# Encoder step on eight cores: the residual add moved to GpSimd, later norm sums and taps, and a DMA transpose of the second group's input

## The chip, the cores and the metric

One program runs on all 8 cores of one Trainium2 chip, each core on its own half of a stream and two of the sixteen running streams; the cores exchange nothing. The metric is the device time of the slowest core in microseconds (us). Engines: TensorE (PE; PEld is its weight load), VectorE (DVE), ScalarE (ACT), GpSimd (POOL), SyncE (SP, which here only issues DMAs).

## What is computed

```
x = x + rmsnorm(merged @ w_out, g_mix_post)          # merged = [normed pooling | normed gated conv]
x = x + rmsnorm(cross_attn(rmsnorm(x, g_x_pre), mem_k, mem_v, w_q, w_co), g_x_post)
hid = jnp.square(jax.nn.relu(rmsnorm(x, g_ff_pre) @ w_up))
x = x + rmsnorm(hid @ w_down, g_ff_post)
```

ahead of it `proj = rmsnorm(x, g_mix_pre) @ w_in`, split into `u | B | C | h`. Pooling: four groups of 128 channels of `u` are averaged over trailing windows of 2, 4, 8, 16 rows, less `u`, and mapped by a 128x128 matrix each. Convolution: `B * conv3(C * h)`, three taps over time per channel. Both are normed by group (128 and 64 channels). The model width is 1024, the hidden width 4096. A core has 2048 prompt rows and 32 rows of running streams.

## The kernel before, in words

The 2048 rows are done in two groups of 8 blocks of 128 rows (`grp` 0 and 1; group 0 has the 32 running rows, `SMP`, as well). A group goes through stage A (`w_in`, mixing), `out_block` with `w_out` for each block, attention (queries, scores, then `out_block` again with the product of values and `w_co`), `w_up`, and `w_down`. Weights come as 512-column pieces into a ring of 6 buffers, loaded through the GpSimd queue as buffers come free.

Order is the order in which the Python code adds instructions: each engine runs its own list in that order, and semaphores are derived from overlaps of what is read and written. A unit is 8 matmuls of one output tile; `tick()` follows it, and `later(n, f)` runs `f` at the n-th tick from then (one more when called outside a tick). So a step put later by one unit stands behind 8 more matmuls on TensorE and behind everything those units add on the others.

Stage A has four phases, each one quarter of `w_in`: U (16 units in group 0), then C, h and B of 12 units each (group 0: three column tiles by four channel groups). `pool_ops` queues the window sums, which are popped after each unit (`pool_some`); `MAP_AT` says after which unit (phase, unit) each pooled tile is mapped (`pool_map`: a matmul into a PSUM bank, a square on ScalarE, then `norm_fin`: the matmul of the norm sums, Ln and Exp on ScalarE, and one tick later a `stt` on VectorE that reads the map's bank and frees it). `bank()` hands out six PSUM banks, the one picked longest ago first. `conv_b` is one tap of the convolution; `conv_some` pops one. `mix_B` multiplies by B and asks for the norm sums of its tile with `later(2, ...)`; `sq_slot` is the buffer of the squares.

`out_block` has 16 matmuls of 512 columns into a pair of banks. Then ScalarE squares the pair with a sum (into `junk`, the bytes of `O`) and makes the factor 1/rms (`rstd`: Ln, Exp); VectorE multiplies by the gain (`tt` into `O`) and adds `O` times the factor to the residual `X` (`stt`). Two ticks later `pre_a` does the next norm: a square of `X` with a sum into `xs`, `rstd`, and the scaling, on ScalarE for every other block and on VectorE for the rest; `pre_b` three ticks later turns it on TensorE (8 transposes) and VectorE puts it into `xT` with its gain.

`stage_down` does the two halves of `w_down` one after the other; `down_evac` ends each block, and in the first half of group 0 `hook0` prepares the 8 blocks of the second group, 8 transposes on TensorE each. A program prints the functions here:

## Time and profile before

| | us |
|---|---|
| three runs, median (lowest to highest) | 898.75 (897.88 to 900.32) |
| the profiled execution | 901.45 |
| its span on the slowest core, core 1 | 900.1 |
| spans of the other cores | 893.8 to 898.5 |
| TensorE busy, core 1 | 859.5 (95%) |
| VectorE, ScalarE, GpSimd busy, core 1 | 448.9, 432.4, 53.0 |

Times in views count from the start of a core's span. Stages of core 1: stage A to 104.5, `w_out` blocks to 142, attention to 262, `w_up` to 380, `w_down` to 475; then the second group, whose stage A ends near 563, its `w_out` blocks near 591, attention near 670. A TensorE that is busy is running matmuls, at the clock granted (PEclk, 1.00 is 2.4 GHz). GpSimd's busy time is only the issue of DMAs.

### The profile page before, as it was taken

What the parts mean: (1) busy time and instruction counts of PE and PEld (TensorE: products, weight loads), DVE (VectorE), ACT (ScalarE), POOL (GpSimd) and SP (SyncE); (2) the same over time, 40 slices, a digit from 0 to 9 for tenths busy, and PEclk for the clock granted to TensorE, in tenths of its full rate; (3) what the DMA queues carried; (4) which work ended last, traced back from release to release, by engine and by line L of the source; (5) the groups of instructions that cost most, each with busy time, mean ns of one, the idle gap of its engine ahead of it and who ended that gap; (6) DMA issues with size and microseconds to landing.
All of it is one profiled execution on the core that took longest, in us unless ns stands there. A gap on an engine that the chain in (4) does not pass through costs nothing.

```text
span 900.1 us, 14693 instructions; the slowest of 8 cores (893.8 to 900.1 us)
## 1 busy us (share of the span) xinstructions
PE 859.5 (95%) x5018; PEld 453.0 (50%) x5018; DVE 448.9 (50%) x772; ACT 432.4 (48%) x1043; POOL 53.0 (6%) x66
## 2 busy tenths in 40 slices
PE   7898898999999999999999998999899999999996
PEld 4565444664456666544444443457454444444442
DVE  3788687476872222232142877886684222200133
ACT  4557888466873333332132386886684333200122
POOL 1100100000000000000001000000000000000000
PEclk9989989999999999999999999999999999999998
DMA  9997376719585654636829992171716746426022
GB/s 195 194 155 110 76 118 105 127 28 206 76 151 81 98 80 62 102 88 115 117 100 120 236 228 82 40 96 23 95 21 110 107 69 94 59 36 87 8 94 94
DMA packets 66793, 91.89 MB, mean 102 GB/s; under 512 B 2936, under 2 KB 58360, under 8 KB 66208
## 3 DMA queue, kind: packets, MB, share of 16 engines
q0 software_dynamic: 58080, 60.95, 48.1%
q1 hardware_dynamic: 8640, 30.00, 10.2%
q8 instruction: 42, 0.69, 0.3%
q14 instruction: 31, 0.25, 0.1%
HBM read 137.49 MB, written 12.30 MB: 166 GB/s over the span
## 4 chain that ended last, share of the span: by engine, by line
PE 80%; ACT 9%; issue 4%; DVE 4%; DMA 2%; ACTq 0%; DVEq 0%; SPq 0%; POOLq 0%
PE psum L393 77%; PE psum L397 3%; ACT stg L411 3%; ACT xsb L411 3%; ACT st L411 2%; ACT un L411 2%; DMA ring<-w_in 1%; DMA X<-xp 1%; DVE un L423 1%; DVE xT L414 1%; DMA conv_p<-stg 1%; DVE X L423 0%; DVE un L414 0%; DVE un L418 0%; DVE xsb L418 0%
## 5 line engine op out<-in xcount | busy, mean ns | idle before, releaser
L393 PE MATMUL psum<-xT,ring 128*128 128x352 bf16 (+6 forms) x2336 | 413.0, 333 | 3.6 <-DVE xT L414 2.5
L393 PEld LDWEIGHTS psum<-xT,ring 128*128 128x128 bf16 x2336 | 226.5, 98 | 167.5 <-issue 6.6
L393 PE MATMUL psum<-ring,un 128*128 128x512 bf16 (+1 forms) x1408 | 302.6, 380 | 0.0
L411 ACT ACTIVATE un<-psum 128x352 bf16<-128x352 f32 (+9 forms) x258 | 125.0, 492 | 201.2 <-PE psum L393 198.9
L393 PEld LDWEIGHTS psum<-ring,un 128*128 128x128 bf16 (+1 forms) x1408 | 130.7, 98 | 157.7 <-issue 9.1
L414 DVE TENSOR_TENSOR un<-un 128x352 bf16<-128x352 bf16 (+5 forms) x176 | 84.8, 483 | 156.8 <-ACT un L411 156.8
L414 DVE TENSOR_TENSOR stg<-psum,gp 128x1024 f32<-128x1024 f32 (+3 forms) x51 | 53.1, 1042 | 106.6 <-ACT stg L411 57.6
L411 ACT ACTIVATE stg<-psum 128x1024 bf16<-128x1024 f32 (+3 forms) x51 | 44.5, 873 | 104.8 <-PE psum L393 102.6
L414 DVE TENSOR_TENSOR xT<-psum,gcs 128x1024 bf16<-128x1024 bf16 (+2 forms) x52 | 60.0, 1155 | 35.7 <-PE psum L397 35.2
L393 PE MATMUL psum<-ring,mg 128*128 128x512 bf16 (+1 forms) x320 | 75.8, 388 | 0.0
L423 DVE SCALAR_TENSOR_TENSOR X<-stg,st,X 128x1024 f32<-128x1024 f32 (+3 forms) x51 | 56.3, 1104 | 6.8 <-DVE stg L414 4.7
L411 ACT ACTIVATE mg<-psum 128x512 f32<-128x512 f32 (+2 forms) x23 | 13.7, 596 | 87.4 <-PE psum L393 71.0
L393 PEld LDWEIGHTS psum<-ring,mg 128*128 128x128 bf16 (+1 forms) x320 | 30.4, 99 | 35.8 <-issue 7.9
L414 DVE TENSOR_TENSOR mg<-psum,gp 128x512 f32<-128x512 f32 (+1 forms) x17 | 11.6, 690 | 60.8 <-ACT mg L411 58.7
L411 ACT ACTIVATE st<-st,epsb 128x1 f32<-128x1 f32 (+2 forms) x105 | 30.9, 295 | 10.3 <-ACT un L411 0.4
L397 PE MATMUL psum<-idb,un 128*128 128x128 bf16 (+2 forms) x288 | 25.3, 217 | 10.7 <-DVE un L418 8.9
L411 ACT ACTIVATE xsb<-X 128x1024 bf16<-128x1024 f32 (+1 forms) x34 | 35.4, 1042 | 0.0
L411 ACT ACTIVATE un<-psum,ast 128x256 bf16<-128x256 f32 (+1 forms) x72 | 33.2, 470 | 1.9 <-DVE ast L430 1.9
L433 DVE TENSOR_REDUCE ast<-psum 128x2 f32<-128x512 f32 (+1 forms) x36 | 24.8, 688 | 17.9 <-PE psum L397 9.0
L397 PE MATMUL psum<-idb,xsb 128*128 128x128 bf16 (+1 forms) x336 | 25.7, 220 | 7.8 <-DVE xsb L418 5.3
L411 ACT ACTIVATE st<-st 128x1 f32<-128x1 f32 (+2 forms) x122 | 26.3, 216 | 11.8 <-ACT st L411 0.8
L397 PEld LDWEIGHTS psum<-idb,xsb 128*128 128x128 bf16 (+1 forms) x336 | 21.1, 99 | 21.0 <-issue 16.5
(95 smaller groups left out, 517.1 us busy)
## 6 DMA issues: line engine op xcount, KB each, us to landing
ring<-w_up POOLq DMA_DIRECT2D x16, 1024.0 KB, 14.2
ring<-w_down POOLq DMA_DIRECT2D x16, 1024.0 KB, 10.7
X<-xp SPq DMA_DIRECT2D x16, 512.0 KB, 14.0
yp<-X SPq DMA_DIRECT2D x16, 512.0 KB, 2.7
ring<-w_in POOLq DMA_DIRECT2D x7, 1024.0 KB, 11.4
ring<-w_out POOLq DMA_DIRECT2D x4, 1024.0 KB, 31.8
ring<-w_q POOLq DMA_DIRECT2D x4, 1024.0 KB, 22.7
stg<-xp SPq DMA_DIRECT2D x8, 512.0 KB, 4.3
```

Of the source, the lines that this page charges most:

```text
L393: P.add("pe", lambda e: e.matmul(out, lhsT=lhsT, rhs=rhs, start=start, stop=stop), reads=[lhsT, rhs], writes=[out])
L397: P.add("pe", lambda e: e.transpose(out=out, in_=in_, identity=idn), reads=[in_, idn], writes=[out])
L411: P.add("act", lambda e: e.activation(out=out, in_=in_, func=func, scale=scale, **kw), reads=rd, writes=wr)
L414: P.add("dve", lambda e: e.tensor_tensor(out=out, in0=in0, in1=in1, op=op), reads=[in0, in1], writes=[out])
L423: P.add("dve", lambda e: e.scalar_tensor_tensor(out=out, in0=in0, scalar=scalar, in1=in1, op0=op0, op1=op1), reads=rd, writes=[out])
L433: P.add("dve", lambda e: e.tensor_reduce(out=out, in_=in_, axis=mybir.AxisListType.X, op=ALU.max, negate=True), reads=[in_], writes=[out])
```

## The change

The residual `X + O * factor` is split: VectorE makes `O = psum * factor * gain` in one `stt` that now needs the factor, and GpSimd adds `O` to `X`. The scaling of `pre_a` in `out_block` is always on VectorE, its square goes to `junk`, and `pre_b` comes a tick later. In stage A the maps of group 0 stand two units apart from unit 5 of phase 1 on, their sums come 2 units later in place of 1, those of the B tiles 3 in place of 2 (both groups), with a fourth square buffer, and taps may run after every unit above 7. The factor of the last norm takes one ScalarE step less in the second half, and the last block leaves in two halves on two queues. In `hook0` the 8 turns go by DMA (SP queue) with the gain applied in place 7 ticks later.

```diff
@@ -283,7 +283,7 @@
 A_TILES = [[(14, 368), (368, 720), (720, 1072)], [(16, 528), (528, 1040)]]
 P_TILES = [[(0, 528), (528, 1072)], [(16, 528), (528, 1040)]]
 P_AT = [(12, 16), (4, 8)]
-MAP_AT = [[[(1, 8), (1, 9), (1, 10), (1, 11)], [(2, 3), (2, 5), (2, 7), (2, 9)], [(2, 11), (3, 0), (3, 2), (3, 4)]],
+MAP_AT = [[[(1, 5), (1, 7), (1, 9), (1, 11)], [(2, 1), (2, 3), (2, 5), (2, 7)], [(2, 9), (2, 11), (3, 1), (3, 3)]],
           [[(1, 4), (1, 5), (1, 6), (1, 7)], [(2, 2), (2, 3), (2, 4), (2, 5)]]]
 F_TILES = [[(16, 368), (368, 720), (720, 1072)], [(16, 528), (528, 1040)]]
 Q_TILES = [F_TILES[0], [(16, 400), (400, 784), (784, 1040)]]
@@ -547,12 +547,12 @@
 
     xs_rr = [0]
 
-    def pre_a(Xap, r, key, on_act=False, xs=None):
+    def pre_a(Xap, r, key, on_act=False, xs=None, junk=None):
         if xs is None:
             k = xs_rr[0] % 2
             xs_rr[0] += 1
             xs = xsb[0:r, k * D:(k + 1) * D]
-        act(xs, Xap, AF.Square, accum=stat(key, 3, r))
+        act(xs if junk is None else junk, Xap, AF.Square, accum=stat(key, 3, r))
         rstd(stat(key, 3, r), stat(key, 4, r), stat(key, 5, r), D)
         if on_act:
             act(xs, Xap, AF.Copy, scale=stat(key, 5, r))
@@ -597,7 +597,7 @@
     sA_OFF = S_OFF
     sB_OFF = [sA_OFF + 16 * w for w in SW]
     SQ_OFF = [sB_OFF[g] + 12 * SW[g] for g in range(2)]
-    RF_OFF = [o + 3072 for o in SQ_OFF]
+    RF_OFF = [SQ_OFF[0] + 3072, SQ_OFF[1] + 4096]
     U3 = uf(U_OFF, 4 * UW).rearrange("p (g t) -> p g t", g=4)
     V3 = uf(V_OFF, 4 * VW).rearrange("p (g t) -> p g t", g=4)
     Z3 = uf(U_OFF, 4 * MW).rearrange("p (g t) -> p g t", g=4)
@@ -689,9 +689,9 @@
             k = map_rr[0] % 4
             map_rr[0] += 1
             return stgb[:, 512 * k:512 * k + n]
-        k = sq_rr[0] % 3
+        k = sq_rr[0] % 4
         sq_rr[0] += 1
-        return ub(SQ_OFF[grp] + 1024 * k, n)
+        return mg[:, 8736:8736 + n] if k == 3 and grp == 0 else ub(SQ_OFF[grp] + 1024 * k, n)
 
     def pool_map(grp, g, lo, hi):
         l1 = max(lo, 16) - 16
@@ -701,7 +701,7 @@
         mm(out, wpool[:, g * 128:(g + 1) * 128], PL3[:, g, l1:h1], True, True)
         sq = sq_slot(grp, n, True)
         act(sq, out, AF.Square, scale=pvt[:, g:g + 1])
-        later(1, lambda: norm_fin(grp, sq, n, ones, 128, out, psg[:, g:g + 1], mg3[:, g, l1:h1]))
+        later(2 if grp == 0 else 1, lambda: norm_fin(grp, sq, n, ones, 128, out, psg[:, g:g + 1], mg3[:, g, l1:h1]))
 
     def conv_a(grp, cc):
         act(Z3[:, cc, 0:NB * 128], V3[:, cc, 0:NB * 128], AF.Copy, scale=WCO(0, cc))
@@ -723,7 +723,7 @@
         tt(y, ps, y, ALU.mult)
         sq = sq_slot(grp, n)
         act(sq, y, AF.Square)
-        later(2, lambda: norm_fin(grp, sq, n, bd64, 64, y, GCO(cc), mg3[:, 4 + cc, lo - 16:hi - 16]))
+        later(3, lambda: norm_fin(grp, sq, n, bd64, 64, y, GCO(cc), mg3[:, 4 + cc, lo - 16:hi - 16]))
 
     def state_out(grp, src, n, dst):
         ms = stg[0:n, D:D + 512]
@@ -801,7 +801,7 @@
                 fill(ph, n, len(units))
                 tick()
                 pool_some(2 if ph == 0 else 1)
-                if grp == 1 or ph == 3 or n % 2 == 1:
+                if grp == 1 or ph == 3 or n % 2 == 1 or n > 7:
                     conv_some()
                 if ph == 3 and n == 3:
                     if grp == 0:
@@ -852,20 +852,19 @@
             if h == 0:
                 weave()
                 tick()
-        par = o_rr[0] % 2 == 0
         k = o_rr[0] % 2
         o_rr[0] += 1
         O = stg[0:r, k * D:(k + 1) * D]
         junk = stgb[0:r, k * 2 * D:k * 2 * D + D]
         act(junk, ps, AF.Square, accum=stat(key, 0, r))
         rstd(stat(key, 0, r), stat(key, 1, r), stat(key, 2, r), D)
-        tt(O, ps, gp[0:r, :], ALU.mult)
+        stt(O, ps, stat(key, 2, r), gp[0:r, :], ALU.mult, ALU.mult)
         xb = Xs(blk)
-        stt(xb, O, stat(key, 2, r), xb, ALU.mult, ALU.add)
+        P.add("pool", lambda e: e.tensor_tensor(out=xb, in0=xb, in1=O, op=ALU.add), reads=[xb, O], writes=[xb])
 
         def p2():
-            xs = pre_a(xb, r, key, par)
-            later(3, lambda: pre_b(xs, r, gi, xT3[:, :, c0 + 16:c0 + 16 + r]))
+            xs = pre_a(xb, r, key, False, None, junk)
+            later(4, lambda: pre_b(xs, r, gi, xT3[:, :, c0 + 16:c0 + 16 + r]))
         later(2, p2)
         weave()
         tick()
@@ -1141,24 +1140,30 @@
         if h == 0:
             O = obuf(b)
             act(O, ps, AF.Square, accum=stat(key, 6, r))
+            act(stat(key, 6, r), stat(key, 6, r), AF.Identity, scale=1.0 / D, bias=epsb[0:r, 0:1])
             tt(O, ps, gp[0:r, 0:512], ALU.mult)
             return
         k = o_rr[0] % 2
         o_rr[0] += 1
         O = stg[0:r, k * D:k * D + 512]
         act(O, ps, AF.Square, accum=stat(key, 7, r))
-        act(stat(key, 0, r), stat(key, 6, r), AF.Identity, bias=stat(key, 7, r))
-        rstd(stat(key, 0, r), stat(key, 1, r), stat(key, 2, r), D)
+        act(stat(key, 1, r), stat(key, 7, r), AF.Ln, scale=1.0 / D, bias=stat(key, 6, r))
+        act(stat(key, 2, r), stat(key, 1, r), AF.Exp, scale=-0.5)
         tt(O, ps, gp[0:r, 512:1024], ALU.mult)
         xb = Xs(b)
 
         def fin():
             stt(xb[:, 0:512], obuf(b), stat(key, 2, r), xb[:, 0:512], ALU.mult, ALU.add)
+            r0 = 0 if b == SMP else (grp * NB + b) * 128
+            last = grp == 1 and b == NB - 1
+            if last:
+                dma("act", yp[r0:r0 + 128, 0:512], xb[:, 0:512], wr=False)
             stt(xb[:, 512:1024], O, stat(key, 2, r), xb[:, 512:1024], ALU.mult, ALU.add)
             if b == SMP:
                 dma("sp", ysm[:, :], xb, wr=False)
+            elif last:
+                dma("sp", yp[r0:r0 + 128, 512:1024], xb[:, 512:1024], wr=False)
             else:
-                r0 = (grp * NB + b) * 128
                 dma("sp", yp[r0:r0 + 128, :], xb, wr=False)
         fin()
 
@@ -1287,7 +1292,9 @@
             xs = pre_a(sl, 128, 12 + j % 2)
             if j + 2 < NB:
                 dma("sp", sl, xrow(1, j + 2), rd=False)
-            later(2, lambda: pre_b(xs, 128, 0, xT3[:, :, xcol(j):xcol(j) + 128]))
+            dst = xT3[:, :, xcol(j):xcol(j) + 128]
+            P.add("sp", lambda e: e.dma_start(out=dst, in_=xs, transpose=True), reads=[xs], writes=[dst], dma=True)
+            later(7, lambda: tt(dst, dst, gcs[:, 0:8].unsqueeze(2).to_broadcast([128, 8, 128]), ALU.mult))
 
     def cache_loads():
         for mc in range(2):
```

TensorE in phase 1 of group 0 (the C units of 8 matmuls 128x352; `un,wpool` is a map, `stg,ones` its norm sums), before:

```order
L393 MATMUL psum<-xT,ring 128x352 x40
L393 MATMUL psum<-un,wpool 128x352
L393 MATMUL psum<-xT,ring 128x352 x8
L393 MATMUL psum<-un,wpool 128x352
L393 MATMUL psum<-stg,ones 128x352
L393 MATMUL psum<-xT,ring 128x352 x8
L393 MATMUL psum<-un,wpool 128x352
L393 MATMUL psum<-stg,ones 128x352
L393 MATMUL psum<-xT,ring 128x352 x8
L393 MATMUL psum<-un,wpool 128x352
```

and in the changed kernel:

```order
L393 MATMUL psum<-xT,ring 128x352 x16
L393 MATMUL psum<-un,wpool 128x352
L393 MATMUL psum<-xT,ring 128x352 x16
L393 MATMUL psum<-un,wpool 128x352
L393 MATMUL psum<-stg,ones 128x352
L393 MATMUL psum<-xT,ring 128x352 x16
L393 MATMUL psum<-un,wpool 128x352
L393 MATMUL psum<-stg,ones 128x352
L393 MATMUL psum<-xT,ring 128x352 x16
L393 MATMUL psum<-un,wpool 128x352
```

The first map stands three units earlier, and a bank is now asked for again between units 9 and 10. VectorE's list is the same up to the first two `mg<-psum` steps that free maps' banks.

VectorE in the `w_out` stage of group 0 (`stg` is `O`, `xsb` the scaled rows, `xT` the turned rows), before:

```order
L414 TENSOR_TENSOR stg<-psum,gp 128x1024
L423 SCALAR_TENSOR_TENSOR X<-stg,st,X 128x1024
L418 TENSOR_SCALAR xsb<-X,st 128x1024
L414 TENSOR_TENSOR xT<-psum,gcs 128x8x128
L414 TENSOR_TENSOR stg<-psum,gp 128x1024
L423 SCALAR_TENSOR_TENSOR X<-stg,st,X 128x1024
L414 TENSOR_TENSOR xT<-psum,gcs 128x8x128
L414 TENSOR_TENSOR stg<-psum,gp 32x1024
L423 SCALAR_TENSOR_TENSOR X<-stg,st,X 32x1024
```

and in the changed kernel:

```order
L423 SCALAR_TENSOR_TENSOR stg<-psum,st,gp 128x1024
L418 TENSOR_SCALAR xsb<-X,st 128x1024
L423 SCALAR_TENSOR_TENSOR stg<-psum,st,gp 128x1024
L414 TENSOR_TENSOR xT<-psum,gcs 128x8x128
L418 TENSOR_SCALAR xsb<-X,st 128x1024
L423 SCALAR_TENSOR_TENSOR stg<-psum,st,gp 32x1024
```

One long step a block is gone from VectorE, and the scaling stands there for every block. SyncE's queue in the `w_down` stage of group 0, as a difference:

```order
-L440 DMA stg<-xp 128x1024 x8
+L440 DMA stg<-xp 128x1024 x3
+L1296 DMA_TRANSPOSE xT<-xsb 128x8x128
+L440 DMA stg<-xp 128x1024
+L1296 DMA_TRANSPOSE xT<-xsb 128x8x128
+L440 DMA stg<-xp 128x1024
```

Each transpose stands behind the load of a later block, and both wait for the scaling of the same block.

## Rows read from the trace of the kernel before

**Rows 1.** The page: busy time by engine, and the TensorE clock in slices.
```profile
PE 859.5 (95%) x5018; PEld 453.0 (50%) x5018; DVE 448.9 (50%) x772; ACT 432.4 (48%) x1043; POOL 53.0 (6%) x66
...
PEclk9989989999999999999999999999999999999998
```

**Rows 2.** TensorE (PE) waits, core 1: line waited for, us in total, times, longest.
```profile
PE psum L397 <- DVE un L418: 8.9, 8, 3.2
PE psum L393 <- ACT un L411: 6.7, 8, 1.8
PE psum L397 <- DVE xsb L418: 5.3, 4, 1.5
...
PE psum L397 <- ACT xsb L411: 2.1, 2, 1.7
```

**Rows 3.** Windows of core 1: busy us (instructions), then clock, DMA share, GB/s.
```profile
61.00:70.00 9.00, 9.00 (x53) 5.49 (x52) 5.32 (x13) 5.40 (x12) 0.87 (x1) 0.82 1.16 162
70.00:104.50 34.50, 28.23 (x182) 16.99 (x181) 28.48 (x57) 27.24 (x58) 0.87 (x1) 1.00 0.50 81
...
800.00:825.00 25.00, 25.00 (x117) 11.33 (x116) 2.77 (x4) 2.75 (x8) 1.39 (x2) 1.00 0.25 35
```

**Rows 4.** Timeline of core 3 around 60 us: start, us, engine [idle before <-releaser].
```profile
56.09 0.31 PE L393 MATMUL psum<-un,wpool 128*128 128x352 bf16 x1
...
60.26 0.80 DVE L423 SCALAR_TENSOR_TENSOR un<-un 128x512 bf16<-128x512 f32 x2
...
60.97 0.58 DVE L423 SCALAR_TENSOR_TENSOR mg<-psum,psg,xsb 128x352 bf16<-128x352 f32 x1
...
61.70 0.31 PE L393 MATMUL psum<-un,wpool 128*128 128x352 bf16 x1 [1.12 <-DVE mg L423]
```

**Rows 5.** Timeline of core 1 in a w_out stage, one block and its neighbours.
```profile
579.48 1.02 ACT L411 ACTIVATE stg<-psum 128x1024 bf16<-128x1024 f32 x1 [0.20 <-PE psum L393]
579.65 0.75 DVE L418 TENSOR_SCALAR xsb<-X,st 128x1024 bf16<-128x1024 f32 x1
580.32 1.22 DVE L414 TENSOR_TENSOR xT<-psum,gcs 128x1024 bf16<-128x1024 bf16 x1
...
581.19 1.04 ACT L411 ACTIVATE xsb<-X 128x1024 bf16<-128x1024 f32 x1
...
581.45 1.22 DVE L414 TENSOR_TENSOR stg<-psum,gp 128x1024 f32<-128x1024 f32 x1
...
582.90 1.28 DVE L423 SCALAR_TENSOR_TENSOR X<-stg,st,X 128x1024 f32<-128x1024 f32 x1 [0.24 <-ACT st L411]
583.09 1.15 ACT L411 ACTIVATE xsb<-X,st 128x1024 bf16<-128x1024 f32 x1
```

**Rows 6.** The page, part 5: the small ScalarE instructions of rstd.
```profile
L411 ACT ACTIVATE st<-st,epsb 128x1 f32<-128x1 f32 (+2 forms) x105 | 30.9, 295 | 10.3 <-ACT un L411 0.4
...
L411 ACT ACTIVATE st<-st 128x1 f32<-128x1 f32 (+2 forms) x122 | 26.3, 216 | 11.8 <-ACT st L411 0.8
```

**Rows 7.** TensorE waits of core 1 between 530 and 563 us.
```profile
PE psum L393 <- ACT un L411: 3.0, 4, 1.6
```

**Rows 8.** Timeline of core 1, w_down of the first group, TensorE.
```profile
412.43 7.07 PE L393 MATMUL psum<-ring,un 128*128 128x512 bf16 x32
...
419.33 0.61 PE L397 MATMUL psum<-idb,xsb 128*128 128x128 bf16 x8
...
419.78 7.07 PE L393 MATMUL psum<-ring,un 128*128 128x512 bf16 x32
```

**Rows 9.** Timeline of core 1, the last block of the kernel.
```profile
893.81 0.29 ACT L411 ACTIVATE st<-st 128x1 f32<-128x1 f32 x1
...
896.03 0.75 DVE L423 SCALAR_TENSOR_TENSOR X<-stg,st,X 128x512 f32<-128x512 f32 x1
```

**Rows 10.** The page, part 6: DMA issues, KB each, us to landing.
```profile
X<-xp SPq DMA_DIRECT2D x16, 512.0 KB, 14.0
yp<-X SPq DMA_DIRECT2D x16, 512.0 KB, 2.7
```


## The prediction

> **What bounds the kernel now.** I read the page first: TensorE is busy 859.5 of 900.1 us, VectorE and ScalarE about half, GpSimd 6% [rows 1]. So a microsecond is won only where matmuls are removed or where TensorE stands still. In w_down, 117 matmuls of 512 columns fill 25.00 us [rows 3], 0.2137 us each, with no idle time: there only less work helps. The view of TensorE's waits says where it stands [rows 2]: 8.9 us for the scaled softmax or the first scaled rows (`un L418`), 6.7 for ScalarE's squares in stage A (`un L411`), 5.3 and 2.1 for the scaled rows that `pre_b` turns (`xsb`). The reader is to see that these are waits for chains across engines, short and many, and that the averages hide dense stretches: in 70 to 104.5 us VectorE is busy 28.48 of 34.5 us and TensorE 28.23 [rows 3]. There neither is full, yet each waits for the other.
>
> **The parts and their prices.** *The turns of `hook0` leave TensorE.* From one run of 32 matmuls to the next it is 419.78 - 412.43 = 7.35 us [rows 8]; 32 x 0.2137 is 6.84, so 8 transposes cost 0.51 us. Eight blocks: **4.1 us** won, where nothing else hides it. The price of a DMA transpose is in no row. Nearest are the SP DMAs of 512 KB: 2.7 us to landing in a quiet stretch, 14.0 in a crowded one [rows 10]. I take 4 us, since w_down is quiet and a block is 256 KB. The cover is 7 ticks: the gain stands 8 units, 13.7 us, behind the hook, and the scaled rows are there after a square, `rstd` and a scaling, some 2.9 us [rows 5, 6]. That leaves 10.8 us for one transpose, and 7.35 us if they go one by one. The in-place gain costs VectorE about what it did, 1.22 us [rows 5].
>
> *Stage A of group 0.* One effect is against the change. A bank comes round after six picks. The map now placed after unit 5 of phase 1 has its bank asked for by the map after unit 9. The step that frees it, `mg<-psum`, stands on VectorE behind all window sums, and on core 3 these run until 60.97; it ends at 61.55. Core 3 already waited 1.12 us for such a step with the old places [rows 4]. Its map after unit 8 ran at 56.09; one more unit (8 x 0.147) and three small matmuls bring the new map to about 57.7, so it waits 3.8 us in place of 1.1, and phase 2 begins 2.7 us later. For the change is what follows. From 70 us on TensorE is idle 6.3 us and VectorE 6.0 [rows 3]: one waits for squares that ScalarE has queued behind a product of VectorE, the other for ScalarE. A sum that comes a unit later (1.2 us, or more) is past most of these waits. Then VectorE's work sets the end: 72.7 + 27.9 (28.48 less one step that moved ahead) + 1.5 of idle time that I leave it = 102.1 in place of 104.5. I take **2.0 us**; with no idle time it is 3.9, and with all 6.0 a loss of 2.1.
>
> *Stage A of group 1* keeps its places and has only later sums and the fourth buffer. Its waits for ScalarE are 3.0 us, none over 1.6 [rows 7], and a unit is 8 x 0.2137 = 1.71 us. At most 3.3 with a small wait for a map's bank, at least 0; I take **2.0**, since VectorE is dense there too.
>
> *The blocks (34 of them).* Before, a block costs VectorE 1.22 + 1.28 + 1.22 and half of 0.75, that is 4.1 us, and ScalarE 1.02 + 1.04 and half of 1.15, two accumulator reads of 0.2 and two `rstd` of 0.5, that is 4.0; TensorE needs 16 x 0.2137 + 0.45 = 3.87 [rows 3, 5, 6, 8]. So ScalarE falls behind a little at each block, and TensorE pays at the ends of the stages, in the `xsb` waits of 7.4 us. After, VectorE has 1.28 + 0.75 + 1.22 = 3.25 and ScalarE 3.45, both below 3.87. Against it, the chain to `X` is longer: the first VectorE step now waits for the factor, 0.6 us, and the add takes p in place of the 1.22 of the old first step. No row has an add on GpSimd. Below, p is at least the 1.28 us of the same shape on VectorE [rows 5]; above, I bound it by 3.9, a block's period, three times that. I take twice, 2.6: the chain grows by 2.0 us. The later `pre_b` gives back a unit, 1.2 to 1.7, and the lag that ScalarE no longer has some more. So I take **4.0** of the 7.4; the ends are -2 (p of 3.9) and 7.4. The Trainium skill (GPSIMD Engine Reference, 3.1) gives 4497 ns for an add of 2048 fp32 columns, so an estimate of 2.25 us here; by it the chain would grow by 1.65 and the sum be some 0.4 us better. No row here shows it.
>
> *Behind the adds on GpSimd's queue* stand weight loads (`w_up`) and four cache loads. They come up to 5 us later than TensorE's last matmul on a buffer; TensorE has no listed wait for a weight on this core, and the ring is ahead by several pieces, so nothing is charged.
>
> *Attention.* VectorE's list has softmax scalings behind the block's steps. The longest wait for them is 3.2 us [rows 2], and the first block step now holds the list 0.6 us longer for the factor, the scaling of rows perhaps for the add. I charge **-1.5**, between 0 and -3.2.
>
> *The end.* One ScalarE step of 0.29 us and its gap leave the last chain, 0.38 us together, and the last transfer is half as long and its first half leaves earlier. From 896.78, the end of the last VectorE step [rows 9], to 900.1 it is 3.3 us. I take **0.7** in all, between 0.4 and 1.5.
>
> Sum: 4.1 + 2.0 + 2.0 + 4.0 - 1.5 + 0.7 = 11.3 us. The profiled execution took 901.45 us, which gives 890.2; it stands 2.7 us over the median, so by the median it is 887.5, rounded to 888.
>
> **The rivals.** *A, the chain eats the rest:* only the turns and the end are won, 4.8 us, and all waits stay, at a longer chain. For it: p is unknown, and 2.0 of growth against 1.2 to 1.7 is not covered by the tick alone. It gives 894.
>
> *B, no difference:* as A, with stage A losing 2.1 and attention 1.5, a net of 1.2 us: 897.5.
>
> *C, the DMA transposes are slow (slower).* If each takes 10 us and they go one by one, the eighth is done 80 us after the first scaling and its gain is due at 7 x 7.35 + 10.8 = 62 us. VectorE, which takes its list in order, stands up to 18 us, and the evacuations behind it stop TensorE when the seven banks are full. With the rest of the sum: 888 + 18 = 906. It decides above 7.35 us each, or 10.8 if they overlap; below it costs nothing. Against it: 256 KB, and 2.7 us for 512 KB when quiet [rows 10].
>
> *D, GpSimd holds VectorE (slower).* VectorE's room in a block is 3.87 - 3.25 = 0.6 us. If its scaling waits half of each add, 1.3 us, a block takes 4.55, and 34 x 0.7 is 24 us: 912. It decides from about 1.0 us a block. An add longer than 3.9 us would do the same by itself. For it: the scaling of 1024 columns takes 0.75 us against 1.22 for steps that read PSUM [rows 5], so it runs in a faster way, and it stands next to the add. Against it: VectorE takes its next step at once where GpSimd must first see a semaphore, so the order mostly favours the scaling. The rule behind this rival is the Trainium skill's (SBUF — State Buffer, Who interferes with whom): VectorE and GpSimd lock a shared pair of ports for a whole instruction, for VectorE's fast modes and for two SBUF inputs. By the rule the old two-SBUF step of 1.28 us would have been the worse partner, and it is gone. No row here shows a collision, since GpSimd computed nothing.
>
> The clock is in none of these: it was granted at 0.82 in 61 to 70 us on core 1 and at 1.00 later [rows 3], and few slices of the page are below 9 [rows 1]. TensorE without its waits could be given such stretches more often; I leave that to the upper end.
>
> **How the numbers follow.** The forecast has 0.58, A 0.17, B 0.10, C 0.08, D 0.07. Less than 0.3% (2.7 us) is about what cannot be told from no change here. Faster is the forecast and A, 0.75; same is B, 0.10; slower is C and D, 0.15. The forecast's own range, with two terms at a time at their ends, is 881 to 893. All best ends together would be 878.5. The range to 899 takes in A and B and leaves C and D and a little below out: 881 to 899.
>
> **What will show it.** Right: 32 matmuls to the next 32 in w_down of group 0 at 6.84 us; eight transposes of under 7 us each; `xsb` waits at about half of 7.4; a new wait for `mg L423` of about 3 us near 60 us on nearly all cores, and the stage's end near 102; adds of 2 to 3 us; VectorE's scaling still at 0.75 us. Wrong: gains on VectorE that wait for a transpose, the `pre_b` waits larger than before, a block period over 3.9 us, or weights that TensorE waits for because their loads stood behind an add. What I trust least is p and the stage A sum, which rests on how much of VectorE's idle time goes.

## The result, and the profile after

| | us |
|---|---|
| changed kernel, median of 4 runs | 920.51 (918.64 to 920.98) |
| kernel before, 4 runs beside it | 899.12 (897.88 to 900.32) |
| ratio, 95% interval | 1.0234 (1.0214 to 1.0254) |
| spans of the profiled execution | 914.4 to 919.3, slowest core 3 |

The change costs 21.4 us; 888 was forecast, with a range of 881 to 899, so the time lies beyond every rival too. Times below are medians of the undisturbed executions (in some, the cores of one half of the chip or both ran at a lower clock and took several per cent longer), which is why a few differ by up to 0.8 us from those that the expectations quote. The page of the slowest core: busy time, the clock in slices, then the two groups of part 5 that the forecast turned on.

```profile
PE 858.8 (93%) x4954; PEld 450.7 (49%) x4954; DVE 460.6 (50%) x755; ACT 417.0 (45%) x1026; POOL 135.8 (15%) x100
...
PEclk9989999999999999999999999999999999999999
...
L863 POOL TENSOR_TENSOR X<-X,stg 128x1024 f32<-128x1024 f32 (+1 forms) x34 | 81.6, 2401 | 100.4 <-DVE stg L423 69.5
...
L418 DVE TENSOR_SCALAR xsb<-X,st 128x1024 bf16<-128x1024 f32 (+1 forms) x34 | 61.1, 1797 | 6.7 <-ACT st L411 6.6
```

Rows 1 are of core 1, so core 3 has to be set beside itself: its TensorE was busy 851.9 of 896.1 us before and is busy 858.8 of 919.3 us now. Of the 23.2 us that its span grew by, 16.3 are idle time; the other 6.9 are busy time, although 64 transposes are gone, so other matmuls ran longer, at a lower clock. The add takes 2.40 us. The scaling `xsb<-X,st`, 0.75 us before [rows 5], has a mean of 1.80. TensorE's waits on core 1 stand against [rows 2]:

```profile
PE psum L397 <- DVE xsb L418: 14.2, 17, 1.7
PE psum L393 <- DVE mg L423: 13.0, 8, 3.8
PE psum L397 <- DVE un L418: 10.6, 10, 3.5
PE psum L393 <- ACT un L411: 4.2, 6, 1.1
```

The waits for ScalarE's squares fell (6.7 to 4.2); those for the scaled rows doubled (7.4 to 14.2), and `mg L423`, the step that frees a map's bank, rose to 13.0. Where they lie shows by stage (us, one profiled execution of each kernel, median of its eight cores, each stage from its first matmul to the next one's; g0 and g1 are the groups; "block part" and so on are the experiments below):

| | before | after | block part | stage A part | turns | transposes one tick later |
|---|---|---|---|---|---|---|
| stage A g0 | 88.1 | 99.1 | 87.5 | 98.2 | 87.8 | 87.8 |
| `w_out` g0 | 36.0 | 39.0 | 37.7 | 37.9 | 36.0 | 35.6 |
| first queries g0 | 16.2 | 18.7 | 18.3 | 15.8 | 16.1 | 19.7 |
| rest of attention g0 | 95.2 | 96.6 | 96.4 | 95.2 | 95.2 | 94.9 |
| `w_up` g0 | 117.9 | 120.1 | 120.2 | 117.9 | 117.9 | 119.3 |
| `w_down` g0 | 122.0 | 117.9 | 121.7 | 121.7 | 118.5 | 121.8 |
| stage A g1 | 65.4 | 64.3 | 65.4 | 64.2 | 65.4 | 65.4 |
| `w_out` g1 | 31.5 | 33.9 | 32.9 | 34.6 | 31.8 | 31.4 |
| attention g1 | 78.6 | 82.4 | 80.5 | 79.2 | 79.3 | 81.7 |
| `w_up` g1 | 112.2 | 111.8 | 111.9 | 112.2 | 112.2 | 113.5 |
| `w_down` g1 and end | 118.0 | 118.5 | 118.1 | 118.0 | 119.4 | 118.0 |

Counted this way core 1's stages before end at 104.7, 141.8, 253.6, 371.5 and 493.5 us, and in the second group at 558.9, 591.1 and 669.9; the 262, 380, 475 and 563 given ahead of the prediction don't fit this count.

Half of the loss is stage A g0. The timeline of core 3 there, changed kernel (columns as in [rows 4]):

```profile
56.69 0.31 PE L393 MATMUL psum<-un,wpool 128*128 128x352 bf16 x1
...
61.90 0.80 DVE L423 SCALAR_TENSOR_TENSOR un<-un 128x512 bf16<-128x512 f32 x2
62.61 0.58 DVE L423 SCALAR_TENSOR_TENSOR mg<-psum,psg,xsb 128x352 bf16<-128x352 f32 x1
...
63.34 0.45 PE L393 MATMUL psum<-un,wpool 128*128 128x352 bf16 x1 [3.80 <-DVE mg L423]
...
63.88 2.55 PE L393 MATMUL psum<-xT,ring 128*128 128x352 bf16 x8
```

The new place of the map makes TensorE wait 3.80 us for `mg<-psum`, which stands behind the window sums (1.12 before, [rows 4]). Then 8 matmuls take 2.55 us, where 16 did before the wait: the clock is at 1.2 GHz. Four more such waits follow (2.57, 0.20, 2.81, 2.27), 11.6 us in the stage against 2.1. Behind the one of 2.57 us the clock stays up, behind the one of 2.81 us it doesn't:

```profile
80.97 2.56 PE L393 MATMUL psum<-xT,ring 128*128 128x354 bf16 x16
...
92.61 4.23 PE L393 MATMUL psum<-xT,ring 128*128 128x352 bf16 x16
```

One window of core 3 over the whole stage, changed kernel and then the kernel before (us, busy by engine, clock, DMA share, GB/s):

```profile
14.70:115.50 100.80, 81.71 (x546) 51.83 (x547) 66.76 (x113) 55.11 (x130) 8.16 (x9) 0.93 0.78 132
```

```profile
14.90:103.50 88.60, 75.48 (x547) 49.34 (x548) 67.19 (x114) 55.69 (x131) 7.87 (x9) 1.00 0.92 150
```

The same matmuls are busy 6.2 us longer, at a mean clock of 0.93 for 1.00, and TensorE is idle 19.1 us for 13.1. So on this core half of the stage's 12.2 us is idle time and half is matmuls at a lower clock. Most of the second half lies behind the waits of 3.80 and 2.81 us; 1.7 us of it lie at 17.26 us, behind a wait of 1.92 us for a weight (28 matmuls in 5.07 us, 3.40 before), ahead of the first map.

In `w_out` g0 the scaling lies beside an add, or doesn't (changed kernel, core 3):

```profile
128.03 2.35 POOL L863 TENSOR_TENSOR X<-X,stg 128x1024 f32<-128x1024 f32 x1 [2.31 <-ACT st L411]
...
128.26 2.67 DVE L418 TENSOR_SCALAR xsb<-X,st 128x1024 bf16<-128x1024 f32 x1 [0.44 <-ACT st L411]
...
131.19 0.61 PE L397 MATMUL psum<-idb,xsb 128*128 128x128 bf16 x8 [0.85 <-DVE xsb L418]
...
132.54 0.74 DVE L418 TENSOR_SCALAR xsb<-X,st 128x1024 bf16<-128x1024 f32 x1
132.83 2.66 POOL L863 TENSOR_TENSOR X<-X,stg 128x1024 f32<-128x1024 f32 x1 [2.45 <-DVE stg L423]
```

The first scaling starts 0.23 us behind an add and takes 2.67 us, until 0.55 us after the add's end; the second starts 0.29 us ahead of an add and takes 0.74. TensorE waits 0.85 us for the first one's rows. By shape, core 3:

```profile
L863 POOL TENSOR_TENSOR X<-X,stg 128x1024 f32<-128x1024 f32 x32 | 76.9, 2405 | 98.5 <-DVE stg L423 67.5 <-DVE mg L427 19.6 <-ACT st L411 11.3
...
L418 DVE TENSOR_SCALAR xsb<-X,st 128x1024 bf16<-128x1024 f32 x32 | 56.6, 1769 | 6.7 <-ACT st L411 6.6
...
L863 POOL TENSOR_TENSOR X<-X,stg 32x1024 f32<-32x1024 f32 x2 | 4.7, 2338 | 1.9 <-DVE stg L423 1.9
L418 DVE TENSOR_SCALAR xsb<-X,st 32x1024 bf16<-32x1024 f32 x2 | 4.5, 2244 | 0.0
```

TensorE's side of the turns went as forecast: no transposes are left in `w_down` g0 (core 1), and a DMA transpose lands 7.2 us after its issue on the median (core 3, 385 to 440 us):

```profile
424.77 20.45 PE L393 MATMUL psum<-ring,un 128*128 128x512 bf16 x94
```

```profile
stg<-xp SPq DMA_DIRECT2D x6, 512.0 KB, 5.1
xT<-xsb SPq DMA_TRANSPOSE x8, 7.2
```

The eight took from 4.7 to 12.4 us, though, and the first gain on VectorE waited for its transpose:

```profile
405.49 1.22 DVE L414 TENSOR_TENSOR xT<-xT,gcs 128x1024 bf16<-128x1024 bf16 x1 [10.51 <-DMA xT<-xsb]
```

VectorE waited 13.2 us so in all, and ScalarE 16.1 us for a buffer of scaled rows (`xsb`) that a transpose still read. TensorE waited for none of it: 152 matmuls run from 389.91 to 418.58 us without a wait.

### The profile page after: what moved, and what is told of

Same layout as the page of the kernel before. It is cut to its first block, busy times and chain, and to the rows that moved or that the text cites. A ratio compares the mean times of both kernels' runs of the same rounds, so it can differ in the third digit from the quotient of the medians.

```text
span 919.3 us, 14741 instructions; the slowest of 8 cores (914.4 to 919.3 us)
## 1 busy us (share of the span) xinstructions
PE 858.8 (93%) x4954; PEld 450.7 (49%) x4954; DVE 460.6 (50%) x755; ACT 417.0 (45%) x1026; POOL 135.8 (15%) x100
## 3 DMA queue, kind: packets, MB, share of 16 engines
q1 hardware_dynamic: 17088, 31.84, 11.6%
## 4 chain that ended last, share of the span: by engine, by line
PE 77%; DVE 8%; ACT 5%; issue 4%; POOL 4%; DMA 2%; DVEq 0%; ACTq 0%; POOLq 0%
PE psum L393 74%; POOL X L863 3%; PE psum L397 3%; ACT un L411 2%; ACT stg L411 2%; DVE stg L423 2%; DVE un L414 2%; DMA ring<-w_in 1%; DVE xsb L418 1%; DVE mg L423 1%; ACT st L411 1%; DVE un L423 1%; DVE xT L414 1%; DVE un L418 0%; ACT xsb L411 0%
## 5 line engine op out<-in xcount | busy, mean ns | idle before, releaser
L863 POOL TENSOR_TENSOR X<-X,stg 128x1024 f32<-128x1024 f32 (+1 forms) x34 | 81.6, 2401 | 100.4 <-DVE stg L423 69.5
L393 PE MATMUL psum<-ring,mg 128*128 128x512 bf16 (+1 forms) x320 | 73.1, 379 | 0.2 <-DVE mg L423 0.2
L418 DVE TENSOR_SCALAR xsb<-X,st 128x1024 bf16<-128x1024 f32 (+1 forms) x34 | 61.1, 1797 | 6.7 <-ACT st L411 6.6
L423 DVE SCALAR_TENSOR_TENSOR stg<-psum,st,gp 128x1024 f32<-128x1024 f32 (+1 forms) x34 | 43.4, 1276 | 28.1 <-ACT st L411 15.4
L414 DVE TENSOR_TENSOR xT<-psum,gcs 128x1024 bf16<-128x1024 bf16 (+2 forms) x44 | 50.1, 1138 | 8.4 <-PE psum L397 7.7
L414 DVE TENSOR_TENSOR stg<-psum,gp 128x512 f32<-128x512 f32 (+1 forms) x17 | 11.7, 686 | 83.6 <-PE psum L393 42.0
L504 POOL DMA_DIRECT2D ring<-w_down x16 | 14.0, 874 | 241.5 <-PE psum L393 241.5
L414 DVE TENSOR_TENSOR mg<-psum,gp 128x512 f32<-128x512 f32 (+1 forms) x17 | 11.7, 690 | 70.3 <-ACT mg L411 66.8
L411 ACT ACTIVATE stg<-X 128x1024 bf16<-128x1024 f32 (+1 forms) x34 | 35.9, 1055 | 23.9 <-POOL X L863 22.4
L397 PE MATMUL psum<-idb,xsb 128*128 128x128 bf16 (+1 forms) x272 | 20.6, 218 | 17.8 <-DVE xsb L418 15.4
```

Source lines behind the costliest of these rows:

```text
L393: P.add("pe", lambda e: e.matmul(out, lhsT=lhsT, rhs=rhs, start=start, stop=stop), reads=[lhsT, rhs], writes=[out])
L397: P.add("pe", lambda e: e.transpose(out=out, in_=in_, identity=idn), reads=[in_, idn], writes=[out])
L411: P.add("act", lambda e: e.activation(out=out, in_=in_, func=func, scale=scale, **kw), reads=rd, writes=wr)
L414: P.add("dve", lambda e: e.tensor_tensor(out=out, in0=in0, in1=in1, op=op), reads=[in0, in1], writes=[out])
L418: P.add("dve", lambda e: e.tensor_scalar(out=out, in0=in0, scalar1=s1, scalar2=None, op0=op0), reads=rd, writes=[out])
L423: P.add("dve", lambda e: e.scalar_tensor_tensor(out=out, in0=in0, scalar=scalar, in1=in1, op0=op0, op1=op1), reads=rd, writes=[out])
```

## The experiments

Each is the kernel before with the edit shown, unless another kernel is named. Ratios are to runs of the kernel before on the same chip, in brackets the 95% interval; microseconds won or lost are the ratio's share of 899.

### The four parts alone

**Block part**: in `out_block` everything that the change did (one `stt`, add on GpSimd, scaling on VectorE, `junk`, `later(4)`). **Stage A part**: `MAP_AT`, map sums two units later, tile sums three, fourth buffer, taps. **Turns**: `hook0`. **End**: `down_evac`. Their diffs are those of the change.

> The kernel before with the block part alone: factor in the first VectorE step, add on GpSimd, all scaling on VectorE, square into the junk bytes, turns one tick later. Theory (GpSimd's adds and VectorE's scaling hold each other up, and the chain over one more engine is longer than the tick it got): the time grows by 13 to 18 us, as the stages of the changed kernel outside stage A and w_down did together (core 3: 2.9 + 2.7 + 1.4 + 2.2 + 1.9 + 0.9 + 4.4 = 16.4), to about 914; the scaling's mean is near 1.8 us in place of 0.77. Rival (the block part only shows what stage A's lateness does to it): within 3 us of before.

Measured: 911.38, 1.0133 (1.0118 to 1.0148).

> The kernel before with the stage A part alone: new places of the maps, their sums 2 units later, sums of the B tiles 3 units later, fourth square buffer, taps after every unit above 7. Theory (a map's PSUM bank is now freed so late that TensorE asks for it again first): about 12 us slower in stage A of group 0 less 1 us in group 1, 909 to 911, with waits for mg L423 of 11 to 12 us and stretches at a lower clock behind the longest. Rival (the stage is late because of something else in the changed kernel, such as DMA traffic): within 3 us of before.

Measured: 913.88, 1.0158 (1.0145 to 1.0172).

> The kernel before with the turns of hook0 as DMA transposes alone. Theory: 4.1 us faster, 895; w_down of group 0 goes from 122.1 to 118 us. Rival (transposes of 7.2 us to landing hold VectorE up or delay weights): no gain.

Measured: 897.03, 0.9975 (0.9964 to 0.9985).

> The kernel before with the end alone: one ScalarE step less per last-half block, the last block in two halves on two queues. Theory: 0.5 to 1 us faster, which is near what can be told apart. Rival: no difference, since the last transfer's fixed part is all that counts.

Measured: 898.46, 0.9989 (0.9979 to 1.0), which can hardly be told from no change.

In ratios that is +12.0, +14.2, -2.2 and -1.0 us of 899, together 23.0 for 21.4 measured: nearly additive, two parts lose and one wins.

### Which half of the block part

The same part with the add on VectorE:

```diff
-        P.add("pool", lambda e: e.tensor_tensor(out=xb, in0=xb, in1=O, op=ALU.add), ...)
+        P.add("dve", lambda e: e.tensor_tensor(out=xb, in0=xb, in1=O, op=ALU.add), ...)
```

> The block part alone, as in the kernel that took 911.4 us (+12.4), but with the residual's add as a tensor_tensor on VectorE instead of GpSimd. Everything else of that part stays: the product and the scale in one step, the squares to a scratch tile, all scaling on VectorE, transposes one later. My theory: the 12.4 us come from GpSimd's add, which holds VectorE's scaling (mean 2.05 us there against 0.77 before) and is itself 2.4 us in the chain where VectorE's own add should be about 1.2. Then the scaling is back near 0.75 us, and the time within 0.4% of before: 896 to 902. Rival, the changed order (all scaling on VectorE, transposes one later, one more VectorE step in the chain) costs by itself: 905 or more with the scaling at 0.75.

Measured: 906.65, 1.0091 (1.0075 to 1.0106), the scaling at 0.75 us. My theory fell: with everything else of the part in place, moving the add to GpSimd costs 3.8 us (1.0133 less 1.0091), a third, and the rest is the order.

With the add on GpSimd and the scaling on ScalarE:

```diff
-            xs = pre_a(xb, r, key, False, None, junk)
+            xs = pre_a(xb, r, key, True, None, junk)
```

> The block part alone with the add on GpSimd, but all scaling of xsb on ScalarE (1.04 us each, as half of it was before), so that no scaling on VectorE lies beside an add. It tells the two halves of my theory apart. If the hold of the scaling (1.3 us more on each) is what costs, most of the 12.4 us goes: 899 to 904. Rival, the 2.4 us add in the chain costs by itself, wherever the scaling is: the chain is then add 2.4 and scaling 1.04, only 1.0 shorter than with the held scaling, and the time stays at 905 to 910. ScalarE, which also has the squares and the copy, could become the one that is waited for (910 or more, with waits for ScalarE's xsb).

Measured: 928.03, 1.0329 (1.0315 to 1.0343), the worst of all. What came is the last case of the expectation: ScalarE is the one that is waited for, so the run doesn't part the hold from the longer add. Core 3's waits, and the last step of the norms of the mixing, on VectorE:

```profile
PE psum L397 <- ACT xsb L411: 17.4, 16, 2.0
...
PE psum L393 <- DVE xT L414: 6.6, 5, 3.0
PE psum L397 <- DVE xT L414: 6.2, 2, 4.9
```

```profile
L423 DVE SCALAR_TENSOR_TENSOR mg<-un,pvt 128x352 bf16<-128x352 f32 (+1 forms) x20 | 17.0, 856 | 7.2 <-ACT un L411 7.0
```

TensorE waits 17.4 us for ScalarE's scaled rows, 2.3 before. The norm step `mg<-un` has a mean of 0.86 us, 0.65 with the add on VectorE: in each group one of them runs beside the first add (two of them take 3.17 us there, 0.58 each elsewhere). That hold is the same 0.86 in the block part alone, so it is no price of moving the scaling.

The old place of the transposes, in the kernel with the add and all scaling on VectorE:

```diff
-            later(4, lambda: pre_b(xs, r, gi, xT3[:, :, c0 + 16:c0 + 16 + r]))
+            later(3, lambda: pre_b(xs, r, gi, xT3[:, :, c0 + 16:c0 + 16 + r]))
```

> The kernel with the block part and the add on VectorE took 906.7 us, +8.2, with each scaling back at 0.75 us, so most of the block part's cost is its order. This is the same with the transposes of a block at their old place, 3 units behind the block, not 4. Theory: with 4, the last blocks' transposes of w_co lie directly ahead of the first w_up unit that reads what they make, so VectorE's gain (1.1 us) is waited for in the open, and TensorE's clock falls behind it (16 matmuls took 4.23 us, normally 2.55). Then most of the 8.2 goes: 897 to 901. Rival, all scaling on VectorE and one step more there (1.23 us) load it too much at the start of w_up, wherever the transposes are: 904 or more.

Measured: 903.06, 1.005 (1.0037 to 1.0062), between theory and rival: the place is somewhat under half of it, 3.7 us. The place alone, the kernel before with 3 changed to 4:

> The kernel before with one number changed: the transposes of a block 4 units behind it instead of 3. By the theory that this place costs by itself, 902 to 907, with the stages that begin behind the blocks (w_up above all) longer and a wait for VectorE's gain of about 1 us in each; in w_out the waits for xsb should shrink. If the cost needs the longer chain too, it is 896 to 900.

Measured: 907.16, 1.0094 (1.0081 to 1.0108). One number costs 8.5 us:

```diff
-            later(3, lambda: pre_b(xs, r, gi, xT3[:, :, c0 + 16:c0 + 16 + r]))
+            later(4, lambda: pre_b(xs, r, gi, xT3[:, :, c0 + 16:c0 + 16 + r]))
```

Its largest wait, core 3, first queries, VectorE and then TensorE:

```profile
145.91 1.22 DVE L414 TENSOR_TENSOR xT<-psum,gcs 128x1024 bf16<-128x1024 bf16 x1
150.67 0.76 DVE L418 TENSOR_SCALAR un<-un,st 128x1024 bf16<-128x1024 f32 x1 [3.54 <-ACT st L411]
151.34 1.22 DVE L414 TENSOR_TENSOR xT<-psum,gcs 128x1024 bf16<-128x1024 bf16 x1
```

```profile
147.82 0.61 PE L397 MATMUL psum<-idb,un 128*128 128x128 bf16 x8
152.71 1.01 PE L397 MATMUL psum<-idb,xsb 128*128 128x128 bf16 x8 [4.28 <-DVE xT L414]
153.52 2.55 PE L393 MATMUL psum<-xT,ring 128*128 128x352 bf16 x8
```

And the same place in the kernel before, core 3, VectorE and then TensorE:

```profile
151.91 0.75 DVE L418 TENSOR_SCALAR un<-un,st 128x1024 bf16<-128x1024 f32 x1 [3.50 <-ACT st L411]
152.58 1.22 DVE L414 TENSOR_TENSOR xT<-psum,gcs 128x1024 bf16<-128x1024 bf16 x1
...
153.94 0.61 PE L397 MATMUL psum<-idb,un 128*128 128x128 bf16 x8 [0.87 <-DVE xT L414]
```

The scaling of the memory's rows (`un<-un,st`) waits 3.5 us for ScalarE in both kernels. Before, one block's gain stood behind it in VectorE's list, and TensorE waited 0.87 us for that. One unit later two gains stand behind it (151.34 and 153.83), the bank of turned rows stays taken when TensorE already wants the next, and TensorE waits 4.28 us; then 8 matmuls take 2.55 us, the slow clock again.

GpSimd's add and nothing else of the block part:

```diff
-        tt(O, ps, gp[0:r, :], ALU.mult)
+        stt(O, ps, stat(key, 2, r), gp[0:r, :], ALU.mult, ALU.mult)
         xb = Xs(blk)
-        stt(xb, O, stat(key, 2, r), xb, ALU.mult, ALU.add)
+        P.add("pool", lambda e: e.tensor_tensor(out=xb, in0=xb, in1=O, op=ALU.add), ...)
```

> The add on GpSimd and nothing else of the block part: product and scale in one step on VectorE, add on GpSimd, scaling in turn on VectorE and ScalarE, squares to xsb, transposes 3 units behind. It gives GpSimd's own share. The chain of a block is 1.2 us longer (add 2.4 instead of 1.2), and VectorE's scaling is held where an add lies beside it. By my theory that this costs 4.7 us (911.4 less 906.7) when the transposes are later, and more when they aren't: 903 to 908. Rival, the add is harmless once the transposes are back: 897 to 900.

Measured: 921.61, 1.0258 (1.0244 to 1.0272), 23.2 us, far outside both cases. Core 3:

```profile
PE psum L397 <- DVE xsb L418: 23.3, 15, 3.8
...
PE psum L397 <- ACT xsb L411: 0.6, 1, 0.6
```

```profile
L864 POOL TENSOR_TENSOR X<-X,stg 128x1024 f32<-128x1024 f32 x32 | 75.5, 2361 | 103.8 <-DVE stg L423 71.2 <-DVE mg L427 19.6 <-ACT st L411 11.7
...
L418 DVE TENSOR_SCALAR xsb<-X,st 128x1024 bf16<-128x1024 f32 x17 | 40.1, 2357 | 10.3 <-ACT st L411 10.3
```

The scalings on VectorE have the length of an add on the mean, 2.36 us, and TensorE waits for the rows that VectorE scaled, hardly for those that ScalarE did. The prices don't add: 23.2 us here, 8.5 for the place, 12.0 for the whole part. It is tempting to say that the later transposes make the add bearable, but this kernel differs from the block part in three things: the place, the engine of half the scalings, and where the squares go. Scaling on ScalarE is dear beside these adds too (29.6 us with all of it there), and no run has the add on GpSimd with only the place put back.

The add on VectorE with scaling in turn and the old place, so that only the fused steps and `junk` are left (`par` and `later(3)` as before):

> The add on VectorE, product and scale in one step, squares to a scratch tile, but scaling in turn on VectorE and ScalarE and transposes 3 units behind, as before. The same with all scaling on VectorE took 903.2, +4.1. If all scaling on VectorE is what costs there, 898 to 900. If the two fused steps in the other order (1.28 and 1.23 us, both behind the ScalarE square, where before the product lay ahead of it) lengthen the chain by about half a microsecond a block at each boundary, 901 to 904.

Measured: 906.57, 1.0061 (1.0048 to 1.0074), and 1.005 with all scaling on VectorE: with the add on VectorE the scaling's engine makes no difference that can be told. The fused `stt` (1.28 us) and the add (1.23) both stand behind the factor, where before the product of 1.22 stood ahead of it; that this is the cause is argued, since `junk` was not parted from it. Against the kernel with the add on GpSimd (1.0258), which differs from this one in the add's engine and in where the squares go, moving the add to GpSimd costs 17.7 us in this order, and 3.8 in the order of the block part.

### Which half of the stage A part

Map sums one unit later again, the rest of the part kept:

```diff
-        later(2 if grp == 0 else 1, lambda: norm_fin(grp, sq, n, ones, 128, ...))
+        later(1, lambda: norm_fin(grp, sq, n, ones, 128, ...))
```

> The stage A part alone, as in the kernel that took 914.2 us (+15.2), but with the map sums one unit later again instead of two; the new places of the maps, the fourth squares buffer, the convolution sums three units later and the moved taps stay. My theory: the bank that a map needs is freed by the step that follows an earlier map's sums, and the second unit of delay pushes that step behind window sums and taps on VectorE. Then the waits for mg fall from 12.9 us to 5 or less and the time to 899 to 904. Rival, the new places alone (maps two units apart) take the banks too early: waits for mg stay over 8 us and the time at 908 or more.

Measured: 908.35, 1.0106 (1.0091 to 1.0122). The unit costs a third of the part's loss, and the waits for `mg` on core 3 went from 12.9 to 4.9: the theory's waits, but the rival's time. In stage A g0 alone it is the most: the stage takes 91.2 us in place of 98.2, where before had 88.1. Only the tile sums and the fourth buffer (`RF_OFF`, `sq_slot` as in the change), all else as before:

```diff
-        later(2, lambda: norm_fin(grp, sq, n, bd64, 64, ...))
+        later(3, lambda: norm_fin(grp, sq, n, bd64, 64, ...))
```

> Of the stage A part only the convolution sums three units later and the fourth squares buffer; maps at their old places, their sums one unit later, taps where they were. If the cost of that part is in the maps' banks alone, this is 897 to 900, at best 1 or 2 us faster, since the sums' matmuls wait less for ScalarE's squares (6.8 us of waits for its un before). Rival, the delayed sums by themselves hold PSUM banks or VectorE's queue: 903 or more with waits for mg above before's 2.4 us.

Measured: 904.14, 1.006 (1.0047 to 1.0072): the rival. Stage A is not longer (87.8 and 64.2), `w_out` is, by 2.3 and 3.5 us. Core 3 around the first block of `w_out` g0, ScalarE and then TensorE:

```profile
109.37 0.50 ACT L411 ACTIVATE un<-un 128x352 f32<-128x352 f32 x1
111.48 0.55 ACT L411 ACTIVATE un<-psum,epsb 128x352 f32<-128x352 f32 x1 [1.61 <-DVE mg L423]
112.13 0.50 ACT L411 ACTIVATE un<-un 128x352 f32<-128x352 f32 x1
112.60 1.02 ACT L411 ACTIVATE stg<-psum 128x1024 bf16<-128x1024 f32 x1
```

```profile
108.60 0.31 PE L393 MATMUL psum<-mg,bd 128*128 128x352 bf16 x1
108.75 7.07 PE L393 MATMUL psum<-ring,mg 128*128 128x512 bf16 x32
117.51 0.61 PE L397 MATMUL psum<-idb,xsb 128*128 128x128 bf16 x8 [1.69 <-ACT xsb L411]
```

The last norm of the mixing is a unit later, so its Ln stands in ScalarE's list ahead of the second block's square and waits 1.61 us for VectorE; that square starts at 112.60, before at 111.42. The chains of the first blocks come late, and TensorE waits 1.69 us for their rows, 0.22 before.

The maps' new places alone (`MAP_AT` and the fourth buffer):

> Stage A with the maps at their new places and nothing else moved but the fourth squares buffer: sums of maps one unit later, convolution sums two, taps where they were. So far the part costs 15.2 us: the convolution sums three units later 5.7 (904.1), then places and taps 4.3 (908.5), then the map sums two units later 5.7 (914.2). If places cost by themselves what they cost there, 902 to 904, with waits for mg above the 2.4 us of before. If maps spread over six units of two quarters only cost where sums are late, 897 to 900.

Measured: 902.28 where before was 900.73, 1.0011 (1.0001 to 1.002). Tile sums `later(3)` with the moved taps, and tile sums `later(3)` with the new places:

> Convolution sums three units later and the moved taps, maps at their old places with sums one unit later. Convolution sums alone cost 0.60%, places alone 0.1%, but with places and taps together it was 1.06%. If the taps make the difference, this is 1.0% slower than before (907 to 909 where before is 899); if not, 0.6% (903 to 905).

Measured: 904.13, 1.0054 (1.004 to 1.0068).

> Convolution sums three units later and maps at their new places with sums one unit later, taps where they were. If places cost only together with the later convolution sums (both put steps ahead of the one that frees a map's bank), 0.9 to 1.1% slower than before, with waits for mg near 5 us on core 3; if the taps were it, 0.6 to 0.7%, with waits near 3.

Measured: 904.63, 1.0049 (1.0036 to 1.0062).

Neither adds anything to the tile sums' 0.6%. Together they do: 1.06%. In the kernel with both (map sums one unit later) stage A g0 is 91.2 us, with either alone 88.0 and 89.0. The waits for `mg` don't tell why: core 3 has one of 2.7 us in 50 to 105 us with the places, three of 4.3 in all with both, and with the taps even more:

```profile
PE psum L393 <- DVE mg L423: 5.6, 4, 2.3
```

By the medians of the cores TensorE is idle 13.2 us in the stage with both, 11.7 with the places and 12.3 with the taps, and busy 78.1 us against 76.8 and 76.7; so about half of what comes on top is matmuls at a lower clock again.

### The turns and the end

One of the 8 turns by DMA:

```diff
+            if j == 0:
+                P.add("sp", lambda e: e.dma_start(out=dst, in_=xs, transpose=True), ...)
+                later(7, lambda: tt(dst, dst, gcs[:, 0:8].unsqueeze(2).to_broadcast([128, 8, 128]), ALU.mult))
+            else:
+                later(2, lambda: pre_b(xs, 128, 0, dst))
```

> Of the 8 block turns in w_down only the first by a DMA transpose. The turns alone took 3.5 us from that stage and only 1.9 from the time; the time from the last X step's end to the span's end was 4.8 us with them and 3.4 without. If that is a price of the program for having any DMA transpose, it is 4.8 here too: 898.5 less 0.4 for the turn plus 1.4, 899 to 900.5. If it grows with the number of them, 3.4 to 3.6 and 898 to 899.

Measured: 900.44 where before was 900.73, 1.0 (0.9991 to 1.001). From the end of VectorE's last step to the end of the span it is 3.1 us here (median of the cores), 3.3 before, 4.7 with eight turns, 4.2 in the changed kernel. So it is no price for having one (or for having the first); between one and eight nothing was run. The last step and the span of one core, eight turns; before they were 889.64 and 893.8 us:

```profile
887.61 0.75 DVE L423 SCALAR_TENSOR_TENSOR X<-stg,st,X 128x512 f32<-128x512 f32 x1
```

```profile
core 4: 893.2 us, clock 0.996
```

### Versions that gain

Turns and end together:

> The two parts of the change that don't cost, together: the 8 block turns by DMA transposes (897.0 us alone) and the shorter end (899.3 alone, no difference). Expected 896 to 897.5. It would beat both kernels if so. The last X step lies 4.8 us before the span's end with the turns by DMA and 3.4 without; if that stays, half a microsecond of the turns' gain is left behind here too.

Measured: 896.0, 0.997 (0.9959 to 0.9982), as expected. And with the new order for the blocks of `w_out` only (`gi == 1`), the add on VectorE:

```diff
+        if gi == 1:
+            stt(O, ps, stat(key, 2, r), gp[0:r, :], ALU.mult, ALU.mult)
+            P.add("dve", lambda e: e.tensor_tensor(out=xb, in0=xb, in1=O, op=ALU.add), ...)
+        else:
...
-            xs = pre_a(xb, r, key, par)
-            later(3, lambda: pre_b(xs, r, gi, xT3[:, :, c0 + 16:c0 + 16 + r]))
+            xs = pre_a(xb, r, key, par and gi != 1, None, junk if gi == 1 else None)
+            later(4 if gi == 1 else 3, lambda: pre_b(xs, r, gi, xT3[:, :, c0 + 16:c0 + 16 + r]))
```

> The version that took 896.0 us (turns by DMA, shorter end) and, for the blocks of w_out alone, the order of the kernel with the add on VectorE: product and scale in one step, VectorE adds, all their scaling on VectorE, transposes 4 units behind; the blocks of w_co as before. In the kernel with that order everywhere (906.7) w_out was 1.1 and 1.2 us shorter and the unit groups behind it 0.3 to 1.0 different, while all the loss lay behind w_co (w_up 3.1, w_co 4.5, w_up 1.2). Expected 893.5 to 896. If the loss comes with the order wherever it is, 897 or more.

Measured: 895.55 where before was 900.73, 0.9947 (0.9935 to 0.996). It is the fastest, 4.8 us by the ratio; its interval and the other's just touch. The two `w_out` stages are 34.9 and 31.0 us, 36.0 and 31.8 without it. With the new order everywhere `w_up` g0 alone took 3.2 us more (121.1 for 117.9), so it wins in `w_out` and loses behind `w_co`.

## Why the prediction was wrong, step by step

- **Turns, 4.1 us.** Right in the stage (122.0 to 117.9 in the changed kernel, 3.5 with the turns alone), but the cover of 7 ticks did not hold throughout: I took 4 us for a transpose, the median is 7.2 and the slowest took 12.4, over the 10.8 that I had. VectorE stood up to 10.5 us for it, the mechanism of rival C and a sign of being wrong that I had named; TensorE waited for none of it, which was luck as much as plan, since the cover had been worked out for shorter transposes. The stage's gain did not all arrive: 1.4 us come back at the end of the span.
- **Stage A of group 0, +2.0 forecast, 11.0 lost.** This is the step that failed most. The wait of 3.8 us at the map after unit 9 came as computed (3.80 on core 3), and the end at 102.1 (itself 2.4 under 104.5, of which I took 2.0) did not: core 1 left the stage at 114.4. I had followed one bank through one re-use and then assumed that sums a unit later only pass waits. They also hold each map's bank a unit longer, and four more maps waited; with the map sums back by one unit 7.0 us of the stage come back. "The clock is in none of these" failed with it: half the loss on core 3 is matmuls at a lower clock, most of it behind these waits. My worry was the other way round, low clock in a TensorE without waits.
- **Stage A of group 1, +2.0 forecast.** The stage gained 1.1, and `w_out` behind it lost 3.1 in the stage A part. I had priced the later sums where they left, not where they arrived, in ScalarE's list between the first blocks.
- **Blocks, +4.0 forecast, 12.0 lost** (with what they do to attention). p was near (2.6 taken, 2.40 measured). "The later `pre_b` gives back a unit" failed: alone it costs 8.5 us, and 3.7 in the longer chain with the add on VectorE. I counted it as slack for the chain and never looked at what stands in the unit it moves into. Rival D was right in its mechanism and not in its weight: the scaling is held until the add ends where it starts behind one, 1.0 us a block on the mean (1.80 less 0.75), its own limit. In the block part alone it is 1.3 us (a mean of 2.05), just what D assumed, and moving the add cost 3.8 us there where D charged 24: the time did not hang on VectorE's load in a block as D had it. My argument against D, that VectorE is ahead by a semaphore, failed: 24 of core 3's 34 scalings took over 1.9 us. The rule of the Trainium skill behind D (SBUF — State Buffer, Who interferes with whom) agrees with these rows, in that the 0.75 us scaling becomes 2.36 beside an add, and that at 132 us, where the scaling is first, it is the add that takes 2.66 us in place of 2.35; that the pair of ports is what is locked no run shows.
- **Attention, -1.5.** Right in sign, far too small: the first queries lose 2.5 us, the rest 1.4, and the second group's attention 3.8, the `w_co` blocks in them included.
- **End, +0.7.** 1.0 us by the ratio, whose interval reaches no gain.
- The Trainium skill's price for the add (GPSIMD Engine Reference, 3.1; estimate 2.25 us) was a little nearer than mine: 2.40 was measured.

What stays open: why taps and places cost only together, why eight DMA transposes lengthen the time from the last step to the end, why the add on GpSimd costs 3.8 us in one order and 17.7 in the other, and map sums two units later at the old places, which was not tried.

## What to carry to other kernels

A step moved one unit later is not slack: read what its new neighbours in each engine's list wait for, and who holds a bank or a buffer that much longer, through every re-use and into the next stage. Before giving an idle engine an elementwise step, ask which steps of the busy engine will run beside it, and give the hold a price even where the average load is low. Price edits alone and together: here the later transposes cost 8.5 us alone and 3.7 in another order of the blocks, and moving the add to GpSimd 3.8 us in one order and 17.7 in another.

## What the runs showed of the hardware that was not expected

- Behind waits of TensorE of 2.81, 3.80 and 4.28 us, matmuls ran at 1.2 GHz for a while: 2.55 us for 8, what 16 took ahead of the wait. Behind one of 2.57 us in the same stage they did not (16 in 2.56 us). In stage A g0 of core 3 matmuls at the lower clock cost 6.2 us, as much as the added idle time.
- A GpSimd add of 32 rows by 1024 takes as long as one of 128 rows (2.34 and 2.41 us), and a VectorE scaling of 32 rows beside it 2.24 us, 0.73 with the add on VectorE.
- DMA transposes of 128 by 1024 bf16 from SBUF to SBUF, in a stage that also loads weights and rows, landed 4.7 to 12.4 us after their issue.
- Eight DMA transposes in the middle of a kernel make the time from its last VectorE step to its end 1.4 us longer; one does not.
